# The scan's decay exponents of a two-layer hybrid decoder, spread over the partitions by loads from DRAM

## What is computed

```
acum = cumsum(dt * a_neg, axis=tokens of the chunk)         # (chunk of 128, 32 heads)
seg  = acum[:, None, :] - acum[None, :, :]                   # t, s, head
decay = exp(where(causal, seg, -inf))
y_diag = einsum('btsg,btsgh,bsghp->btghp', cb, decay, xdt)   # cb = C B^T of a group
```

## Time and profile before

| | us |
|---|---|
| runs, three | 1540.09, 1540.17, 1542.2 (median 1540.17) |
| the profiled execution | 1541.87 |
| its span, first to last instruction | 1540.1 |
| TensorE busy | 1407.9 (91%) |
| VectorE busy | 849.5 (55%) |
| ScalarE busy | 382.8 (25%) |
| GpSimd busy | 75.7 (5%) |
| mean granted TensorE clock | 0.966 |

### The profile page before, as it was taken

How to read it: one execution, slowest core, us unless ns; L and a number is a source line. 1 busy time by engine, 2 the same in 40 slices (tenths; PEclk the granted TensorE clock), 3 DMA queues, 4 the chain that set the end, 5 groups by cost and what they waited for, 6 DMA issues and landing times.

```text
span 1540.1 us, 24221 instructions
## 1 busy us (share of the span) xinstructions
PE 1407.9 (91%) x9794; PEld 1118.5 (73%) x9794; DVE 849.5 (55%) x1611; ACT 382.8 (25%) x875; POOL 75.7 (5%) x65
## 2 busy tenths in 40 slices
PE   8999999999999998777799999999999999887684
PEld 7888888899998563334288888888999985534241
DVE  5487878677974341212165787786688643321022
ACT  2222457411111121001122234575021021110011
POOL 0000520000000000000000015100000000000000
PEclk9999999999999999888999999999999999998898
DMA  8434223336551689999963343333384508899995
GB/s 311 156 143 147 96 108 119 117 125 249 186 169 55 273 327 418 419 416 416 381 233 142 132 164 111 109 111 110 110 300 164 169 1 342 354 420 416 416 417 243
DMA packets 115711, 350.12 MB, mean 227 GB/s; under 512 B 11664, under 2 KB 13968, under 8 KB 99216
## 3 DMA queue, kind: packets, MB, share of 16 engines
q1 hardware_dynamic: 115056, 346.47, 58.5%
q0 software_dynamic: 544, 2.10, 0.3%
HBM read 347.50 MB, written 1.05 MB: 226 GB/s over the span
## 4 chain that ended last, share of the span: by engine, by line
PE 77%; DMA 17%; DVE 3%; ACT 1%; issue 1%; SPq 0%; DVEq 0%; POOL 0%; POOLq 0%; ACTq 0%
PE bank L838 21%; PE bank L841 17%; PE bank L807 13%; DMA wring<-in_w_up_e 8%; DMA ga<-in_w_down_e 8%; PE bank L788 5%; PE bank L1163 5%; PE bank L1125 3%; PE bank L764 3%; PE bank L961 2%; PE bank L1217 2%; PE bank L1200 1%; PE bank L1050 1%; PE bank L950 1%; PE bank L986 1%
## 5 line engine op out<-in xcount | busy, mean ns | idle before, releaser
L807 PE MATMUL bank<-hT,wring 128*128 128x256 f32 x896 | 196.2, 380 | 0.0
L807 PEld LDWEIGHTS bank<-hT,wring 128*128 128x128 f32 x896 | 169.5, 190 | 23.7 <-issue 0.7
L1163 PE MATMUL bank<-wring,big 128*32 128x256 f32 x1536 | 108.7, 446 | 37.7 <-DMA wring<-in_w_up_e 23.0
L1163 PEld LDWEIGHTS bank<-wring,big 128*32 128x32 f32 x1536 | 54.2, 127 | 90.4 <-issue 25.7
L2122 DVE TENSOR_TENSOR h<-bank,h 128x512 f32<-128x512 f32 x64 | 44.3, 692 | 115.7 <-PE bank L1217 115.7
L2113 DVE TENSOR_TENSOR big<-bank,big 128x256 f32<-128x256 f32 x16 | 6.8, 425 | 164.3 <-ACT big L1462 164.3
L1718 DVE SCALAR_TENSOR_TENSOR scr<-bank,prm,scr 128x255 f32<-128x255 f32 (+1 forms) x144 | 62.7, 477 | 47.5 <-ACT scr L1283 44.8
L838 PE MATMUL bank<-big,wring 128*128 128x128 f32 x704 | 84.3, 282 | 3.8 <-ACT big L1315 3.8
L838 PE MATMUL bank<-hT,wring 128*128 128x128 f32 x736 | 86.9, 276 | 0.8 <-DVE btok L1579 0.8
L838 PEld LDWEIGHTS bank<-hT,wring 128*128 128x128 f32 x736 | 84.2, 192 | 3.4 <-issue 2.1
L838 PEld LDWEIGHTS bank<-big,wring 128*128 128x128 f32 x704 | 83.1, 199 | 4.3 <-issue 4.2
(11 more groups left out here) (359 smaller groups left out, 2358.5 us busy)
## 6 DMA issues: line engine op xcount, KB each, us to landing
wring<-in_w_in SPq DMA_DIRECT2D x68, 1024.0 KB, 7.0
wring<-in_w_gate_e SPq DMA_DIRECT2D x16, 4096.0 KB, 20.7
wring<-in_w_up_e SPq DMA_DIRECT2D x16, 4096.0 KB, 21.9
wring<-in_w_ssd_o SPq DMA_DIRECT2D x16, 1024.0 KB, 6.5
wring<-in_w_ckv SPq DMA_DIRECT2D x16, 1024.0 KB, 7.4
scr<-in_w_down_e SPq DMA_DIRECT2D x8, 2048.0 KB, 28.8
ga<-in_w_down_e SPq DMA_DIRECT2D x8, 2048.0 KB, 31.0
qq<-in_w_down_e SPq DMA_DIRECT2D x8, 2048.0 KB, 26.4
```

Of the source, the lines that this page charges most:

```text
L807: ins = nc.tensor.matmul(bank[bank_of(job)][:, i * SEQ:(i + 1) * SEQ], wring[:, SLOT[c], k, m:m + P], src[:, k, :], start=n == 0, stop=n = ...
L1163: ins = nc.tensor.matmul(bank[b][j * S:(j + 1) * S, i * F:(i + 1) * F], x[:, k, e:e + S], up_part[i][:, j, k * F:(k + 1) * F], start=k == ...
```

## The change

The 128 transposes of repeated columns go. In their place TensorE transposes `acum` once a layer (a new step `acumT` behind kiT: two transposes, 128 tokens x 32 heads each, into one bank), VectorE copies the result (32 partitions x 256) into columns of `rt`, and SyncE stores it to a DRAM array `acum_rows`, ahead of the chunk of xbc 4. For each n of the scan SyncE then loads 8 heads x 128 values, one row of 4 KB, into all 128 partitions of a `mm_` buffer. The loads stand in SyncE's queue ahead of the chunk of z 2 (load 0) and of the four gate chunks (loads 1 and 2, 3 and 4, 5 and 6, and 7). Load 0 waits for the stored rows and for the last Silu of the convolution, load 1 for the roped queries, load n for the filling of `ssd n-2`. ScalarE does its Relus in place in SBUF and has a semaphore between them and the Exp. The two `mm_` buffers are exchanged ((n + 1) % 2).

```
@@ make_order, JOBS_OF
-    o += [... ("acum",), ("kT",), ("kiT",), ("xbc", 0), ("qiT", 0), ("qiT", 1), ("xbc", 1)]
+    o += [... ("acum",), ("kT",), ("kiT",), ("acumT",), ("xbc", 0), ("qiT", 0), ("qiT", 1), ("xbc", 1)]
-    "decay": (2, "act"),
+    "acumT": (1, "dve"),
@@ SyncE
+            def save_acum(l):
+
+                drained(sp, l, JOB[(("acumT",), 0)])
+                settle(sp)
+                sp.dma_start(acum_rows[l].rearrange("t h s -> h t s"), acum_turned).then_inc(ac_saved, 16)
+
+            def acum_to_all(l, n):
+
+                t, g = SSD[n]
+                if n == 0:
+                    sp.wait_ge(ac_saved, l * 16 + 16)
+                    settle(sp)
+                    sp.wait_ge(silu_rdy, l * 12 + 12)
+                elif n == 1:
+                    sp.wait_ge(q_rdy, l * 2 + 2)
+                else:
+                    filled(sp, l, JOB[(("ssd", n - 2), 0)])
+                settle(sp)
+                row = acum_rows[l, t, g * HG:(g + 1) * HG, :].rearrange("h s -> (h s)")
+                sp.dma_start(mm_[:, (n + 1) % 2, :], bc(row, 0, P)).then_inc(dec_in[n % 2], 16)
...
+                z0 = CHUNK[(("z", 0), 0)]
+                ahead_of = {z0 + 2: (0,), z0 + 4: (1, 2), z0 + 5: (3, 4), z0 + 6: (5, 6), z0 + 7: (7,)}
                 for c in range(NCH):
+                    if c == CHUNK[(("xbc", 4), 0)]:
+                        save_acum(l)
+                    for n in ahead_of.get(c, ()):
+                        acum_to_all(l, n)
                     chunk(l, c, before)
@@ TensorE
-                elif kind == "decay":
-
-                    t, g = SSD[st[1]]
-                    drained(pe, l, JOB[(("acum",), 0)])
-                    for j in range(2):
-                        job = JOB[(st, j)]
-                        free(l, job)
-                        for i in range(4):
-                            hd = g * HG + 4 * j + i
-                            ins = nc.tensor.transpose(bank[bank_of(job)][:, i * P:(i + 1) * P],
-                                                      acum[:, t, hd:hd + 1].to_broadcast([P, P]), ident)
-                        ins.then_inc(filled_s, 1)
+                elif kind == "acumT":
+
+                    pe.wait_ge(ac_rdy, l + 1)
+                    job = JOB[(st, 0)]
+                    free(l, job)
+                    for t in range(TT):
+                        ins = nc.tensor.transpose(bank[bank_of(job)][0:SH, t * P:(t + 1) * P], acum[:, t, :], ident)
+                    ins.then_inc(filled_s, 1)
@@ ScalarE, decay
-                    if n == 0:
-                        act.wait_ge(silu_rdy, l * 12 + 12)
-                    if n >= 2:
-                        filled(act, l, JOB[(("ssd", n - 2), 0)])
-                    for j in range(2):
-                        job = JOB[(st, j)]
-                        filled(act, l, job)
-                        for i in range(4):
-                            hd = 4 * j + i
-                            ins = nc.scalar.activation(mm_[:, n % 2, hd * P:(hd + 1) * P], bank[bank_of(job)][:, i * P:(i + 1) * P],
-                                                       ACT.Relu, bias=acum[:, t, g * HG + hd:g * HG + hd + 1], scale=-1.0)
-                        drain_inc(ins, job)
-                    drained(act, l, job)
-                    nc.scalar.activation(mm_[:, n % 2, :], mm_[:, n % 2, :], ACT.Exp, scale=-1.0).then_inc(dec_rdy, 1)
+                    act.wait_ge(dec_in[n % 2], (l * (len(SSD) // 2) + (n // 2 + 1)) * 16)
+                    for hd in range(HG):
+                        m = mm_[:, (n + 1) % 2, hd * P:(hd + 1) * P]
+                        ins = nc.scalar.activation(m, m, ACT.Relu, bias=acum[:, t, g * HG + hd:g * HG + hd + 1], scale=-1.0)
+                    ins.then_inc(seg_rdy, 1)
+                    act.wait_ge(seg_rdy, l * len(SSD) + (n + 1))
+                    m = mm_[:, (n + 1) % 2, :]
+                    nc.scalar.activation(m, m, ACT.Exp, scale=-1.0).then_inc(dec_rdy, 1)
@@ VectorE
+                elif kind == "acumT":
+                    filled(dve, l, job)
+                    drain_inc(V.tensor_copy(acum_turned, b[0:SH, 0:SEQ].rearrange("p (t s) -> p t s", t=TT)), job)
```

More of the change, by code:

```diff
@@ L89, in make_order @@
     o = [("norm", 0)] + [("hT", 0, i) for i in range(4)]
-    o += [("small",), ("sums", "h0"), ("kv",), ("dt",), ("qi",), ("acum",), ("kT",), ("kiT",), ("xbc", 0), ("qiT", 0), ("qiT", 1), ("xbc", 1)]
+    o += [("small",), ("sums", "h0"), ("kv",), ("dt",), ("qi",), ("acum",), ("kT",), ("kiT",), ("acumT",), ("xbc", 0), ("qiT", 0), ("qiT", 1), ("xbc", 1)]
     o += [("idx", 0, 0), ("topk", 0), ("xbc", 2)]
@@ L156 @@
     "acum": (1, "dve"), "kT": (1, "dve"), "kiT": (1, "dve"), "qiT": (1, "act"), "idx": (2, "act"),
-    "xT": (1, "act"), "bT": (1, "act"), "cb": (1, "dve"), "qT": (1, "act"), "decay": (2, "act"),
+    "xT": (1, "act"), "bT": (1, "act"), "cb": (1, "dve"), "qT": (1, "act"), "acumT": (1, "dve"),
     "score": (2, "dve"), "probT": (1, "act"), "pv": (1, "act"), "whole_gate": (2, "act"),
@@ L311, in trunk @@
         acum = sb("acum", [P, 3, SH])
+        acum_rows = nc.dram_tensor("acum_rows", (DEPTH, TT, SH, P), F32).ap()
         eac = sb("eac", [P, SH])
@@ L443, in trunk @@
         rw = btok[:, :].rearrange("p (k n) -> p k n", k=KC)[:, :, 0:G + G * E]
+        acum_turned = cols(rt, R_MR, TT, P)[0:SH]
         bank = [ctx.enter_context(nc.psum_tensor(f"bank{b}", [P, NCOL], F32)) for b in range(8)]
@@ L476, in trunk @@
         ac_rdy = sem("acum_ready")
+        ac_saved = sem("acum_turned_stored")
+        dec_in = [sem(f"acum_rows_in{i}") for i in range(2)]
         eac_rdy = sem("exp_acum_ready")
@@ L479, in trunk @@
         x_scaled = sem("x_scaled")
+        seg_rdy = sem("decay_exponents_ready")
         dec_rdy = sem("decay_ready")
@@ L961, in stage @@
                         ins = nc.tensor.matmul(bank[bank_of(job)][:, i * SP_:(i + 1) * SP_],
[L962 removed]
+                                               mm_[:, (n + 1) % 2, i * P:(i + 1) * P],
                                                xdt[:, n % 2, i * SP_:(i + 1) * SP_], start=True, stop=True)
@@ L1787, in stage @@
                     dve.wait_ge(dec_rdy, l * len(SSD) + (n + 1))
-                    m3 = mm_[:, n % 2, :].rearrange("p (h t) -> p h t", h=HG)
+                    m3 = mm_[:, (n + 1) % 2, :].rearrange("p (h t) -> p h t", h=HG)
                     V.tensor_tensor(m3, m3, bc(cbm[:, t, g * P:(g + 1) * P], 1, HG), ALU.mult).then_inc(m_rdy, 1)
```

## The result

| | before | after |
|---|---|---|
| median of six runs | 1539.92 us | 1546.06 us (1543.74 to 1547.05) |
| ratio, with its 95% interval | | 1.0036 [1.0024, 1.0048] |
| the profiled execution, its span | 1541.87, 1540.1 | 1546.93, 1545.1 |
| TensorE busy | 1407.9 | 1394.1 |
| mean granted clock | 0.966 | 0.969 |

A forecast was written before the change was run, and what follows sets the result against it. TensorE, without idle time in the changed stretch, was taken to bound the kernel: 7.0 - 4.7 - 0.9 - 0.4 = 1.0 us shorter a layer, giving 1538.2, plus 2.8 for one clock loss: 1541.0; range 1535.6 to 1545.5.

The forecast's parts named there:

- The clock term: TensorE's clock falls to half behind the new wait ahead of acumT in one of two layers, losing 2.8 us.
- rival 1: Both layers' waits ahead of acumT cost the clock, 2 x 2.8 us: 1543.8 us, slower by 3.6; chance 0.22.
- the same: Outcome within about 0.2% of the kernel before, 1537.1 to 1543.3 us; chance 0.50.
- slower: Outcome above 1543.3 us; chance 0.30.
- the wait of 3.46 us: Existing TensorE wait at 741.79 us, clock still 1.00 behind it; taken as evidence against a clock loss.
- the row at 710.81: Existing TensorE wait of 4.81 us, then 5.55 us of work at half speed; taken as 2.8 us lost.
- The wait: TensorE waits ahead of acumT and the first xbc product for VectorE's subtraction: 4.7 us a layer lost.
- The removal: Eight decay groups of transposes leave TensorE's scan, 8 x 0.88 = 7.0 us a layer saved.
- the two give-backs: TensorE waits for late masks at the first and eighth scan products: 0.9 and 0.4 us a layer given back.
- The loads: The 512 KB loads land in 5.8 us, delay no weight chunk; load 1's mask holds by 0.7 us.
- Rivals 3 and 4: Slower: load 1 lands late, 1548.8, chance 0.10; or a wait for the decay through SBUF replaces the transposes, 1549.6, chance 0.05.
- Rival 2: Scan masks do not come late, nothing is given back and no clock lost: 1535.6 us; chance 0.13.

The follow-up runs named there:

- the second, 1544.65: The changed kernel measured and profiled once more, unedited: 1544.65 us, ratio 1.003 to the kernel before.
- the trace with 20 transposes: The changed kernel with 20 identity transposes on TensorE ahead of its wait for the sum, leaving 2.1 us idle: 1540.39 us.
- the wait alone: The kernel before, with only a TensorE wait for VectorE's sum added ahead of the first xbc product: 1551.85 us, ratio 1.0076.
- the kernel with q's transposes in the gap: Changed kernel with acumT behind the first xbc product, plus q 0/1 transposes before the first scan product and two z Silus behind decay 7: 1526.94 us.
- that with 1.03: The changed kernel with 30 identity transposes on TensorE ahead of its wait for the sum: 1540.18 us, ratio 0.9996.

## Why the terms of the prediction held and its likeliest case did not

**The clock term failed.** The step reads: "so I take one loss in the two layers as the likeliest: 1538.2 + 2.8 = 1541.0". Both layers lost it, in all three traces with a wait of 4.3 us and in the one with 2.1. This is rival 1, 1543.8, which I gave 0.22. The first measurement, 1546.06, lies 0.6 us above the end of the range, with an interval that reaches into it; the second, 1544.65, lies within. I had given "the same" 0.50 and "slower" 0.30, and it was slower. That the 1543.8 of rival 1 comes near to 1544.65 is in part luck: its 5.6 us of clock were 3.6 and 3.8, and the rest of the time measured lies in none of its terms. What misled me was the wait of 3.46 us with the clock at 1.00 behind it: I read the two rows as points on one scale of idle time and put 4.4 between them. At this place, in one profiled execution each, 1.0 us of idle time lost nothing, and 2.1 lost about as much as 4.3; old waits of 1.90 and 2.48 us lost in some executions and not in others. The length of the wait alone does not decide. Why the wait at 741.79 was spared stays open; its own place was not varied. The Trainium skill, "TensorE: Matmul & The Clock Gate", section "HAM oscillation — how this bites in real kernels", names a length of wait beyond which the work that follows starts cold. Here that held after 4.3 us of idle time in six cases of six. In the trace with 20 transposes it held after 2.1 us as well, a shorter wait than the page names; it did not after 1.0.

**Its size was off the other way.** I took 2.8 us from the row at 710.81. Measured were 1.4 to 2.4 with the change and up to 2.6 with the wait alone. The half-speed work in layer 1 goes from 40.71 to about 44.9, since 0.77 of full speed over 44 to 46 leaves 0.9 of it at 0.50. That is 4.2 us of work, and half of it is lost, against 5.55 us at 710.81. Part of the slow stretch lay in the idle time, where it costs nothing. In layer 2 the slow stretch was shorter: 0.53 and 0.62 of full speed over 806 to 810 leave 3.4 us at 0.50, all of it in work, and 1.7 lost.

**The wait was right.** 4.7 us a layer forecast, 4.87 and 4.70 measured, released by VectorE's subtraction in both. The wait alone shows the same 4.29 us of idle time.

**The removal was right.** 7.0 less the two give-backs is 5.7 a layer, measured 5.24 and 5.22. At the first mask 0.9 came back, as forecast: the z group ahead of it began at 163.52 and lets go after 3.45, and the scan product began at 167.91, 0.94 later. It goes when other work stands there. At the last mask 0.67 came back in place of 0.4. My step took 9.65 us of ScalarE's and VectorE's chain as it stood; with the change the eight Relus, which read SBUF in place of PSUM, take 2.43 us where they took 2.15. That is 0.27 of the 0.5 us missing from the sum. Most of the rest lies in the scan products behind the two waits: from their start to the next group it is 1.81 and 1.80 us, where it was 1.73 and 1.74.

**The loads were right.** Taken at 5.8 us, bounded by 3.1 and 10.3; landed in 3.4 to 7.5, median 4.1. The second scan product does not wait for load 1, TensorE waits for no weight chunk in the scan, and fourteen of the sixteen loads could go without a gain. Rivals 3 and 4 are refuted: the scan has two waits a layer, and both stay the same where no load is made. Rival 2 needed VectorE's backlog to shrink; it did not by itself, but the kernel with q's transposes in the gap shows that TensorE need not wait for it.

## What to carry to other kernels

Before a new step is put into the instruction stream of the busiest engine, look up when its input is ready, and put it behind the next piece of work that needs nothing new: here one place in the list turned 0.36% lost into 0.63% gained. On TensorE count a wait of 4 us among dense work as its length and the clock behind it in every layer. Where one spared wait in a trace speaks against that, do not average, but take it as unexplained. For a shorter wait ask more than one execution. And measure a wait by the starts of the groups around it, since the idle time in a bracket leaves out part of it.

## What the runs showed of the hardware that I had not expected

- In one profiled execution TensorE's clock fell behind 2.12 us of idle time in both layers, as behind 4.3 (15.65 and 15.66 us for 64 products in layer 2). In that with 1.03 it did not. By the medians of the two kernels (1540.39 and 1540.18 us) most executions with 2.12 lost less. With 2.12 it fell only once work was under way again. The windows of that kernel, layer 1, with the products from 41.26 on:

```profile
40.00:42.00 2.00, 0.97 (x6) 0.88 (x7) 1.70 (x6) 0.35 (x2) 0.00 (x0) 1.00 1.05 401
42.00:44.00 2.00, 2.00 (x7) 1.62 (x6) 0.23 (x1) 0.00 (x0) 0.00 (x0) 0.54 0.29 95
44.00:46.00 2.00, 2.00 (x8) 1.59 (x7) 0.00 (x0) 0.00 (x0) 0.00 (x0) 0.61 0.00 0
```

- 4.3 us of transposes of a constant kept the clock at its upper level as well as products did: 13.98 us behind 38 of them in both layers.
- One row of 4 KB read by all 128 partitions, 512 KB in all, landed in 4.1 us at the median, 1.0 us later than 512 KB stored from SBUF (3.1).
- Old waits of 1.90 and 2.48 us lower the clock in some executions and not in others, 1.6 and 1.2 us each time, and a load of 1 MB that lands 1.2 us late comes with 0.9 to 1.2 us more on the path. Differences of 1 to 2 us between two single profiles of this kernel mean nothing until the step is named in which they arise.
